# Window attention: the exponentials' product with the values in rounded parts, and one step later

## The chip, the cores and the metric

The kernel runs on one core of a Trainium2 chip. The metric is the device time of one execution in microseconds. TensorE is the matmul engine, VectorE, ScalarE and GpSimd the three elementwise ones, SyncE issues the transfers. The profile writes PE, DVE, ACT, POOL and SP for them, and PEld for TensorE's weight loads.

## The reference, cut to what matters

The model is a chain of blocks: an RWKV-7 time mixing, a stick-breaking attention, a window attention and a short convolution, each followed by a gated feed-forward network (f0 to f3). The change is in the window attention. It has 16 query heads of 64 features over 4 key and value heads, 512 tokens, and 256 context tokens that every query sees. Queries go in blocks of 128. A block of queries sees the keys at most 128 positions away, and a learned logit (the sink) takes part in the softmax without a value.

```python
def gqa_softmax(q, k, v, mask, sink):
    s = jnp.einsum('bkgqd,bkjd->bkgqj', q, k, preferred_element_type=jnp.float32) * (q.shape[-1] ** -0.5)
    if mask is not None:
        s = jnp.where(mask, s, NEG)
    ...
        sk = sink.astype(jnp.float32)[None, :, :, None, None]
        m = jnp.maximum(s.max(axis=-1, keepdims=True), sk)
        e = jnp.exp(s - m)
        p = e / (e.sum(axis=-1, keepdims=True) + jnp.exp(sk - m))
    return jnp.einsum('bkgqj,bkjd->bkgqd', p.astype(v.dtype), v)
```

## The kernel before

Activations lie with features on the partitions and tokens in the columns. A linear layer (`lin_pe`, L325) keeps weights and activations as two tensors of TensorE's rounded type: the rounded value (`hi`) and the rest (`lo`, the value minus its rounded value), and sums three products, hi by hi, hi by lo and lo by hi. ScalarE rounds each weight chunk (L295), VectorE makes its rest (L302). A matmul of plain `F32` tensors needs no such parts; the trace shows two records for each.

**The window attention** (L2491 to L2720) goes through 16 groups, one for each key head `kv` and query block `qb`. A group handles four query heads at once, 4 x 128 = 512 columns. It has `NQ` key blocks of 128: two of the context and two or three of the neighbourhood, so 4, 5, 5, 4 for the four `qb`. All engines follow one list written out by hand, `WATT` (L2520), in which every engine finds its own part of each step:

- `max` (g, j): TensorE makes the scores of head j of group g with queries on the partitions (L2572 to L2581, 512 or 640 columns), VectorE takes the maximum (L2670). It runs one group ahead. Two areas of PSUM take turns, so a `max` waits for VectorE's reduce two before it (L2570).
- `shift` (g): VectorE forms the negative maximum, bounded by the sink (L2679), and four diagonal matrices of it (L2683).
- `key` (g, q): TensorE makes the scores of key block q with keys on the partitions, from rounded keys and their rests (L2599, L2600), adds the mask where there is one (L2602) and the shift (L2605). ScalarE takes the exponential into `Pw` (L2643), `F32`, three buffers. The key step q = NQ gives the sink's part (L2592), whose exponential (L2636) goes into `dn`.
- `val` (g, q): TensorE multiplies `vw` by `Pw` (L2611). `vw` (L2093) holds 64 columns of values and 64 columns of ones, so the product gives both the weighted values and the sum of the exponentials. `vw` and `Pw` are `F32`. The value columns are written by ScalarE from PSUM (L2423), the ones by a GpSimd memset (L2480).
- `end` (g, 0..3): VectorE adds the denominators (L2691), ScalarE inverts them by Ln and Exp (L2649, L2651), VectorE normalises (L2697, two instructions), ScalarE rounds (L2655) and GpSimd makes the rest (L2719). In groups 5 to 12 VectorE also scales one part of the residual stream in `end` 3 (L2707).
- `queries` (g), in groups 0 to 3: ScalarE and VectorE split two more query blocks of the rotary embedding (`rope_hi`, `rope_lo`, L2373).

The list for step `_q` of a group puts `key`, then the next group's `max`, then `end` of the group before, then `val` of the key block one before:

```python
                WATT.append(("key", _g, _q))
                if _g + 1 < NG and _q < 4:
                    WATT.append(("max", _g + 1, _q))
                    ...
                if _g and _q < 4:
                    WATT.append(("end", _g - 1, _q))
                if _q:
                    WATT.append(("val", _g, _q - 1))
```

Each engine's queue is in order. VectorE's first instruction of the stage is L2660, TensorE's is the first `max` (L2572), which waits for ScalarE's last value copy. The output projection (`wino`) starts when GpSimd has the last rest (L2617).

Of the kernel before, what the change touches and what calls it, by code (L numbers as in the profile page):

```python
# [7 lines left out]
F32 = mybir.dt.float32  # L8
F32R = mybir.dt.float32r
# [228 lines left out]
def program(nc, d_h, d_ctx, d_vec, d_cst, d_csr, d_csb, d_csw, d_slc, d_w, d_ada, d_cond, d_out):  # L238
    with ExitStack() as ctx:
# [3 lines left out]
        def sig(name, order):  # L243
            return Sig(sem(name), order)
# [21 lines left out]
        def v(name, i=0, n=1):  # L266
            o = VEC[name] + i
            return vec[:, o:o + n]
# [206 lines left out]
        class Squares:  # L475
# [9 lines left out]
            def rest(self, e):  # L485
                e.preload_act_table_set("natural_log_exp_and_others")
                rms_square(e, self.t, self.src, self.sq, self.there, (6, 7))
# [1605 lines left out]
        vw = mem.left("vw", [128, 6, 4, 128])  # L2093
# [21 lines left out]
        r1 = mem.left("r1", [128, LX])  # L2115
        mem.lo = cx0
# [350 lines left out]
        def win_pool(e):  # L2467
# [12 lines left out]
            e.memset(vw[:, :, :, 64:128], 1.0).then_inc(*zeroed.up("vw", 0))  # L2480
# [15 lines left out]
        NP = 3  # L2496
        Pw = mem.left("Pw", [128, NP, 512])
        nmr = mem.left("nmr", [128, 2, 4], F32R)
# [4 lines left out]
        on = mem.left("on", [128, 2, 2, 128])  # L2503
        flatp = psum[:, :, :].rearrange("p b c -> p (b c)")
# [16 lines left out]
        for _g in range(NG):  # L2521
            for _q in range(NQ[_g] + 1):

                WATT.append(("key", _g, _q))
                if _g + 1 < NG and _q < 4:
                    WATT.append(("max", _g + 1, _q))
                    if _q == 3:
                        WATT.append(("shift", _g + 1, 0))
                if _g and _q < 4:
                    WATT.append(("end", _g - 1, _q))  # L2530
                if _q:
                    WATT.append(("val", _g, _q - 1))
            if _g < 4:

                WATT.append(("queries", _g, 6 + _g))
        WATT += [("end", NG - 1, q) for q in range(4)]
# [13 lines left out]
        t_p = sig("t_p", wk("key"))  # L2550
        t_v = sig("t_v", [(g, q) for g, q in wk("val")])
# [4 lines left out]

        def watt_pe(e):
            e.wait_ge(*q_v.at(2))
            for s, g, q in WATT:
# [46 lines left out]
                elif s == "val":  # L2606
                    b, n = 6 + g % 2, pkey[g, q]
                    e.wait_ge(*t_p.at(g, q))
                    if q == 0 and g >= 2:
                        e.wait_ge(*t_o.at(g - 2, 1))  # L2610
                    ins = e.matmul(psum[:, b, :], vw[:, ts_[q][0], kv, :], Pw[:, n % NP, :], start=q == 0, stop=q == NQ[g] - 1,  # L2611
                                   skip_group_check=True)
                    ins.then_inc(*t_v.up(g, q))
# [6 lines left out]
        def watt_act(e):  # L2620
# [4 lines left out]
            for s, g, q in WATT:  # L2625
# [4 lines left out]
                elif s == "key":  # L2630
# [10 lines left out]
                    if m >= NP:  # L2641
                        e.wait_ge(*t_v.at(*keys_[m - NP]))
# [15 lines left out]
        def watt_dve(e):  # L2658
            e.wait_ge(*w_used.at(last_chunk("winv", 0)))
            e.tensor_scalar(ns8[:, :], v("sink", 0, 16), -8.0, None, ALU.mult).then_inc(*t_n8.up(0))  # L2660
            for s, g, q in WATT:
# [22 lines left out]
                elif s == "queries":  # L2684
                    rope_lo(e, q)
                elif s == "end":
# [25 lines left out]
        def watt_pool(e):  # L2712
            for s, g, q in WATT:
                kv, qb = groups[g]
                i = g % 2
                if s == "end" and q == 3:
                    cs_ = slice(128 * qb, 128 * qb + 128)
                    e.wait_ge(*t_oh.at(g))
                    e.tensor_tensor(XoW.lo[:, 2 * kv:2 * kv + 2, cs_], on[:, i, :, :],  # L2719
                                    XoW.hi[:, 2 * kv:2 * kv + 2, cs_].bitcast(F32), ALU.subtract).then_inc(*t_ol.up(g))  # L2720
# [329 lines left out]
```

## Time and profile before

| | us |
|---|---|
| three runs | 3118.66 median (3114.68 to 3126.62) |
| the profiled execution, its own time | 3126.0 |
| its span in the profile | 3124.2 |
| TensorE busy | 3029.7 (97%) |
| VectorE busy | 1822.9 (58%) |
| ScalarE busy | 1309.7 (42%) |
| GpSimd busy | 519.5 (17%) |

The profile is of one execution. A span is counted from its first instruction. Busy time of TensorE is modelled: matmuls overlap in its pipeline, so the distance from one start to the next says more on the cost of a pass than its duration does. The window attention lies at about 1960 to 2125 us. The granted clock is a share of TensorE's full speed.

### The profile page before, as it was taken

The numbers are of one execution on the slowest core, as the hardware profiler recorded it, in microseconds if no ns is written. First come the engines' busy times: TensorE is split into PE (matmuls) and PEld (weight loads), VectorE is DVE, ScalarE is ACT, GpSimd is POOL, SyncE is SP. The second block draws the span as 40 slices with busy tenths as digits, with TensorE's granted clock in tenths as the row PEclk, the third lists the DMA queues.
The fourth block names the chain that finished last, engine by engine and source line by source line (L and its number), as shares of the span: only waits on it lengthen the run. The fifth ranks groups of instructions, "written<-read, shape, count | busy, mean of one in ns | idle before, by whom it ended". The sixth has DMA issues, their size and how long they took to land.

```text
span 3124.2 us, 46510 instructions
## 1 busy us (share of the span) xinstructions
PE 3029.7 (97%) x19324; PEld 2667.5 (85%) x19324; DVE 1822.9 (58%) x2664; ACT 1309.7 (42%) x2229; POOL 519.5 (17%) x464
## 2 busy tenths in 40 slices
PE   6999999999999999999999999998999999999999
PEld 6987878799999989998999987666888878878887
DVE  7675545448858563563876865664544543365353
ACT  4464555524323254673322355553332332343232
POOL 0002222123203200001311322101211201112020
PEclk9899989899999999999999999999999999999999
DMA  3210000014545422003554542101222222223222
GB/s 107 77 50 35 1 1 1 36 48 169 185 154 188 131 103 88 8 1 130 183 183 163 180 153 68 41 1 54 95 95 88 93 91 94 97 79 98 86 93 94
DMA packets 79554, 284.32 MB, mean 91 GB/s; under 512 B 8528, under 2 KB 9296, under 8 KB 78576
## 3 DMA queue, kind: packets, MB, share of 16 engines
q1 hardware_dynamic: 79344, 281.35, 27.1%
q8 instruction: 153, 2.51, 0.3%
q14 instruction: 57, 0.47, 0.1%
HBM read 274.96 MB, written 6.36 MB: 90 GB/s over the span
## 4 chain that ended last, share of the span: by engine, by line
PE 92%; DVE 4%; ACT 2%; issue 1%; DMA 0%; POOL 0%; SPq 0%; DVEq 0%; ACTq 0%; POOLq 0%
PE psum L345 64%; PE psum L2611 2%; PE psum L1193 2%; PE psum L839 2%; PE psum L1783 2%; PE psum L1214 2%; PE psum L1984 2%; PE psum L1225 1%; PE psum L1222 1%; PE psum L1966 1%; PE psum L1957 1%; PE psum L782 1%; DVE xt L682 1%; PE psum L2605 1%; PE psum L503 1%
## 5 line engine op out<-in xcount | busy, mean ns | idle before, releaser
L302 DVE TENSOR_TENSOR wlo<-wraw,whi 128x1024 fp32r<-128x1024 f32 (+2 forms) x398 | 508.6, 1299 | 629.7 <-ACT whi L295 620.6
L295 ACT CAST whi<-wraw 128x1024 fp32r<-128x1024 f32 (+2 forms) x398 | 396.2, 1022 | 515.4 <-PE psum L345 483.5
L426 DVE CUSTOM_DVE_ANT_0 araw<-araw,cond 128x1024 f32<-128x1024 f32 x112 | 181.2, 1655 | 0.0
L345 PE MATMUL psum<-f0xh,whi 128*128 128x264 f32 x704 | 143.8, 286 | 5.5 <-DVE f0xl L540 3.9
L345 PE MATMUL psum<-f1xh,whi 128*128 128x258 f32 x704 | 142.4, 284 | 5.6 <-DVE f1xl L540 3.8
L345 PE MATMUL psum<-f2xh,whi 128*128 128x512 f32 x352 | 140.1, 398 | 4.2 <-DVE f2xl L536 4.2
L345 PE MATMUL psum<-f3xh,whi 128*128 128x512 f32 x352 | 139.9, 397 | 4.2 <-DVE f3xl L536 4.2
L345 PE MATMUL psum<-f0xh,wlo 128*128 128x264 f32 x704 | 143.4, 285 | 0.0
L345 PE MATMUL psum<-f0xl,whi 128*128 128x264 f32 x704 | 143.0, 285 | 0.0
L345 PE MATMUL psum<-f1xh,wlo 128*128 128x258 f32 x704 | 142.3, 284 | 0.0
L345 PE MATMUL psum<-f1xl,whi 128*128 128x258 f32 x704 | 141.9, 283 | 0.0
L345 PE MATMUL psum<-f2xl,whi 128*128 128x512 f32 x352 | 139.9, 397 | 0.0
L345 PE MATMUL psum<-f2xh,wlo 128*128 128x512 f32 x352 | 139.7, 397 | 0.0
L345 PE MATMUL psum<-f3xl,whi 128*128 128x512 f32 x352 | 139.6, 397 | 0.0
L345 PE MATMUL psum<-f3xh,wlo 128*128 128x512 f32 x352 | 139.5, 396 | 0.0
L1301 ACT ACTIVATE XX<-psum 128x512 fp32r<-128x512 f32 (+2 forms) x216 | 109.4, 519 | 31.1 <-PE psum L1225 25.2
L1345 DVE TENSOR_TENSOR WW<-psum,csr 128x256 fp32r<-128x256 f32 (+1 forms) x216 | 84.0, 395 | 54.7 <-PE psum L1214 53.3
L345 PEld LDWEIGHTS psum<-f0xh,whi 128*128 128x128 f32 x704 | 109.8, 190 | 6.1 <-issue 4.3
L345 PEld LDWEIGHTS psum<-f1xh,whi 128*128 128x128 f32 x704 | 109.6, 191 | 6.2 <-issue 4.2
L345 PEld LDWEIGHTS psum<-f1xh,wlo 128*128 128x128 f32 x704 | 109.7, 190 | 0.0
L345 PEld LDWEIGHTS psum<-f0xh,wlo 128*128 128x128 f32 x704 | 109.6, 190 | 0.0
L345 PEld LDWEIGHTS psum<-f0xl,whi 128*128 128x128 f32 x704 | 109.5, 189 | 0.0
(509 smaller groups left out, 8605.7 us busy)
## 6 DMA issues: line engine op xcount, KB each, us to landing
wraw<-d_w SPq DMA_DIRECT2D x357, 512.0 KB, 3.3
araw<-d_ada SPq DMA_DIRECT2D x112, 512.0 KB, 3.3
wraw<-d_w SPq DMA_DIRECT2D x32, 384.0 KB, 3.4
hn<-d_h SPq DMA_DIRECT2D x4, 528.0 KB, 7.6
hres<-d_h SPq DMA_DIRECT2D x1, 2112.0 KB, 8.5
spill<-hres SPq DMA_DIRECT2D x1, 2112.0 KB, 7.4
hres<-spill SPq DMA_DIRECT2D x1, 2112.0 KB, 9.1
cond<-d_cond SPq DMA_DIRECT2D x2, 1024.0 KB, 4.8
```

Of the source, the lines that this page charges most:

```text
L295: e.copy(whi[0:rows, n % NH, 0:kt * cols], wraw[0:rows, n % NR, 0:kt * cols]).then_inc(*w_hi.up(n))
L302: e.tensor_tensor(wlo[0:rows, n % NH, 0:kt * cols], wraw[0:rows, n % NR, 0:kt * cols], whi[0:rows, n % NH, 0:kt * cols].bitcast(F32), ALU. ...
L345: ins = e.matmul(psum[0:bw, b0 + nb * len(sl) + si, 0:ln], l_ if z == 2 else h_, (xp.lo if z == 1 else xp.hi)[:, k, o:o + ln], start=k == ...
L426: e.tensor_tensor_reduce(out=w, in0=w, in1=self.c[:, col, :], scale=1.0, scalar=0.0, op0=ALU.mult, op1=ALU.add, accum_out=ada[:, ly, blk, ...
L839: ins = e.matmul(psum[0:ln, b, 256 * (ti % 2):256 * (ti % 2) + 256], a_, w_[:, i, :], start=k == 0 and z == 0 and ti % 2 == 0, stop=k == 7 ...
L1193: ins = e.matmul((p1, p0)[w].rearrange("p (a t) -> p a t", a=4)[:, :, 0:T], src[:, blk, q.tok], q.Zp[:, :, 0:T], start=True, stop=True)
L1214: ins = e.matmul(p1[:, 128 * j:128 * j + T], q.Ar[0:T, j, 0:T], q.X[0:T, j, 0:T], start=True, stop=True)
L1301: e.activation(q.X[0:T, o:4, 0:T], p0.rearrange("p (j x) -> p j x", j=4)[:, o:4, 0:T], ACT.Copy).then_inc(*c_xe.up(blk, c, s[1]))
L1345: e.tensor_tensor(q.W[0:T, :, 0:T], p1[:, 0:256].rearrange("p (j x) -> p j x", j=2)[:, :, 0:T], q.bc(lv(s[1])), ALU.mult).then_inc(*c_we.u ...
L1783: ins = e.matmul(psum[0:ln, b, 256 * (ti % 2):256 * (ti % 2) + 256], a_, w_[:, k - k0, :], start=k == 0 and z == 0 and ti % 2 == 0, stop=k ...
L1984: ins = e.matmul(psum[:, 6 + half, lo_ - a0:hi_ - a0], vz, wtt[:, w % 2, col + lo_ - a:col + hi_ - a], start=kb == 2 and hh % 2 == 0, stop ...
L2611: ins = e.matmul(psum[:, b, :], vw[:, ts_[q][0], kv, :], Pw[:, n % NP, :], start=q == 0, stop=q == NQ[g] - 1, skip_group_check=True)
```

## The change

The value product is made of three rounded passes. `vw` becomes a rounded tensor, and VectorE makes its rest `vwl` in three subtractions from PSUM, and zeros for the columns of ones (rest of 1 is 0), ahead of its part of the list. GpSimd copies each exponential into a rounded tensor `Ph` (four buffers), VectorE subtracts it from `Pw` into `Pl` (four buffers), and TensorE multiplies `vw` by `Ph`, `vwl` by `Ph` and `vw` by `Pl`. The exponentials' buffer is free when its rest is made; a copy waits for the value product four blocks back. The list gets a part `rest`, `val` follows its scores by two key blocks in place of one, and all but the fourth `end` move one step later. GpSimd's columns of ones become a copy, and it makes the rest of the heads' outputs (`rest(g - 2)`) before the first copy of a group.

```diff
@@ -2090,7 +2090,7 @@
         mem.lo = sb0
-        vw = mem.left("vw", [128, 6, 4, 128])
+        vw = mem.left("vw", [128, 6, 4, 128], F32R)
         csw = mem.left("csw", [128, NCSW])
@@ -2477,7 +2478,8 @@
             e.wait_ge(*w_ss.at("B"))
-            e.memset(vw[:, :, :, 64:128], 1.0).then_inc(*zeroed.up("vw", 0))
+            e.tensor_copy(vw[:, :, :, 64:128].rearrange("p t h x -> p (t h) x"),
+                          ones[:, 0:64].unsqueeze(1).broadcast_to((128, 24, 64))).then_inc(*zeroed.up("vw", 0))
             for n in range(10):
@@ -2493,14 +2495,24 @@
         ns8 = mem.left("ns8", [128, 16])
-        NP = 3
+
+        NP, NPR = 3, 4
         Pw = mem.left("Pw", [128, NP, 512])
+        Ph = mem.left("Ph", [128, NPR, 512], F32R)
         nmr = mem.left("nmr", [128, 2, 4], F32R)
 ...
         on = mem.left("on", [128, 2, 2, 128])
+        assert mem.lo <= wx1
+
+        mem.lo = cx0
+        vwl = mem.left("vwl", [128, 6, 4, 128], F32R)
+        Pl0 = mem.left("Pl0", [128, 2, 512], F32R)
+        assert mem.lo <= rp0
+        mem.lo = rp1
+        Pl1 = mem.left("Pl1", [128, 2, 512], F32R)
         flatp = psum[:, :, :].rearrange("p b c -> p (b c)")
@@ -2526,14 +2538,18 @@
                         WATT.append(("shift", _g + 1, 0))
-                if _g and _q < 4:
-                    WATT.append(("end", _g - 1, _q))
+                if _g and _q == 0:
+                    WATT.append(("val", _g - 1, NQ[_g - 1] - 1))
+                if _g and _q:
+                    WATT += [("end", _g - 1, x) for x in ((_q - 1,) if _q < 4 else (3,) if _q == 4 else ())]
                 if _q:
-                    WATT.append(("val", _g, _q - 1))
+                    WATT.append(("rest", _g, _q - 1))
+                if _q > 1:
+                    WATT.append(("val", _g, _q - 2))
             if _g < 4:
 ...
                 WATT.append(("queries", _g, 6 + _g))
-        WATT += [("end", NG - 1, q) for q in range(4)]
+        WATT += [("val", NG - 1, NQ[-1] - 1)] + [("end", NG - 1, q) for q in range(4)]
         wk = lambda name: [(g, q) for s, g, q in WATT if s == name]
@@ -2548,14 +2564,21 @@
         t_p = sig("t_p", wk("key"))
+        t_ph = sig("t_ph", keys_)
+        t_pl = sig("t_pl", wk("rest"))
+        t_vl = sig("t_vl", [(b,) for b in range(4)])
         t_v = sig("t_v", [(g, q) for g, q in wk("val")])
 ...
 
+        def Pl(n):
+            return (Pl1 if n % NPR >= 2 else Pl0)[:, n % 2, :]
+
         def watt_pe(e):
             e.wait_ge(*q_v.at(2))
+            e.wait_ge(*t_vl.at(2))
             for s, g, q in WATT:
@@ -2604,13 +2627,17 @@
                 elif s == "val":
-                    b, n = 6 + g % 2, pkey[g, q]
-                    e.wait_ge(*t_p.at(g, q))
+                    b, n, t = 6 + g % 2, pkey[g, q], ts_[q][0]
+                    if n == 0:
+                        e.wait_ge(*t_vl.at(3))
+                    e.wait_ge(*t_ph.at(g, q))
                     if q == 0 and g >= 2:
                         e.wait_ge(*t_o.at(g - 2, 1))
-                    ins = e.matmul(psum[:, b, :], vw[:, ts_[q][0], kv, :], Pw[:, n % NP, :], start=q == 0, stop=q == NQ[g] - 1,
-                                   skip_group_check=True)
-                    ins.then_inc(*t_v.up(g, q))
+                    e.matmul(psum[:, b, :], vw[:, t, kv, :], Ph[:, n % NPR, :], start=q == 0, stop=False, skip_group_check=True)
+                    e.matmul(psum[:, b, :], vwl[:, t, kv, :], Ph[:, n % NPR, :], start=False, stop=False, skip_group_check=True)
+                    e.wait_ge(*t_pl.at(g, q))
+                    e.matmul(psum[:, b, :], vw[:, t, kv, :], Pl(n), start=False, stop=q == NQ[g] - 1,
+                             skip_group_check=True).then_inc(*t_v.up(g, q))
 
@@ -2639,7 +2666,7 @@
                     if m >= NP:
-                        e.wait_ge(*t_v.at(*keys_[m - NP]))
+                        e.wait_ge(*t_pl.at(*keys_[m - NP]))
                     e.activation(Pw[:, m % NP, :], psum[:, 4 + n % 2, :], ACT.Exp, scale=0.125).then_inc(*t_p.up(g, q))
@@ -2658,6 +2685,13 @@
             e.tensor_scalar(ns8[:, :], v("sink", 0, 16), -8.0, None, ALU.mult).then_inc(*t_n8.up(0))
+
+            for b in range(3):
+                e.wait_ge(*q_v.at(b))
+                e.tensor_tensor(vwl[:, 2 * b:2 * b + 2, :, 0:64], psum[:, b, :].rearrange("p (t h x) -> p t h x", t=2, h=4),
+                                vw[:, 2 * b:2 * b + 2, :, 0:64].bitcast(F32), ALU.subtract).then_inc(*t_vl.up(b))
+            e.tensor_scalar(vwl[:, :, :, 64:128].rearrange("p t h x -> p (t h) x"),
+                            ones[:, 0:64].unsqueeze(1).broadcast_to((128, 24, 64)), 0.0, None, ALU.mult).then_inc(*t_vl.up(3))
             for s, g, q in WATT:
@@ -2683,6 +2717,12 @@
                     rope_lo(e, q)
+                elif s == "rest":
+                    n = pkey[g, q]
+                    e.wait_ge(*t_ph.at(g, q))
+                    if n >= NPR:
+                        e.wait_ge(*t_v.at(*keys_[n - NPR]))
+                    e.tensor_tensor(Pl(n), Pw[:, n % NP, :], Ph[:, n % NPR, :].bitcast(F32), ALU.subtract).then_inc(*t_pl.up(g, q))
                 elif s == "end":
@@ -2710,14 +2750,22 @@
         def watt_pool(e):
-            for s, g, q in WATT:
+            def rest(g):
                 kv, qb = groups[g]
-                i = g % 2
-                if s == "end" and q == 3:
-                    cs_ = slice(128 * qb, 128 * qb + 128)
-                    e.wait_ge(*t_oh.at(g))
-                    e.tensor_tensor(XoW.lo[:, 2 * kv:2 * kv + 2, cs_], on[:, i, :, :],
-                                    XoW.hi[:, 2 * kv:2 * kv + 2, cs_].bitcast(F32), ALU.subtract).then_inc(*t_ol.up(g))
+                cs_ = slice(128 * qb, 128 * qb + 128)
+                e.wait_ge(*t_oh.at(g))
+                e.tensor_tensor(XoW.lo[:, 2 * kv:2 * kv + 2, cs_], on[:, g % 2, :, :],
+                                XoW.hi[:, 2 * kv:2 * kv + 2, cs_].bitcast(F32), ALU.subtract).then_inc(*t_ol.up(g))
+
+            for n, (g, q) in enumerate(keys_):
+                if q == 0 and g >= 2:
+                    rest(g - 2)
+                e.wait_ge(*t_p.at(g, q))
+                if n >= NPR:
+                    e.wait_ge(*t_v.at(*keys_[n - NPR]))
+                e.tensor_copy(Ph[:, n % NPR, :], Pw[:, n % NP, :]).then_inc(*t_ph.up(g, q))
+            rest(NG - 2)
+            rest(NG - 1)
 
```

The hunk left out only keeps an address (`rp1`).

## Rows read from the trace of the kernel before

**Rows 1.** Busy per engine in the stage: length, PE, PEld, DVE, ACT, POOL, clock.
```profile
1967.00:2121.00 154.00, 152.92 (x642) 104.55 (x642) 99.79 (x198) 88.35 (x189) 11.00 (x15) 0.98 0.06 21
```

**Rows 2.** Waits in the stage: us in total, times, longest.
```profile
DVE mxw L2670 <- PE psum L2581: 37.5, 42, 2.7
```

**Rows 3.** Line L2592: durations in ns, first and last start.
```profile
L2592 PE MATMUL psum<-dg,oR x16: 792/793/799, 1977.1 to 2118.9; 128*128 128x512 f32 x16
```

**Rows 4.** TensorE's timeline, one step: start us, us, line.
```profile
2031.45 0.39 PE L2602 MATMUL psum<-mk,iR 128*128 128x512 f32 x1
2031.68 0.39 PE L2605 MATMUL psum<-dg,oR 128*128 128x512 f32 x1
2031.90 0.28 PE L2572 MATMUL psum<-Kh,Qx 128*128 128x256 f32 x1
...
2032.20 1.07 PE L2611 MATMUL psum<-Pw,vw 128*128 128x512 f32 x2
...
2033.57 0.39 PE L2605 MATMUL psum<-dg,oR 128*128 128x512 f32 x1
```

**Rows 5.** VectorE's groups from 1966 to 2121, by form: busy us, mean ns.
```profile
L2670 DVE TENSOR_REDUCE mxw<-psum 128x1 f32<-128x640 f32 x32 | 26.4, 824 | 19.8 <-PE psum L2581 19.6
L2670 DVE TENSOR_REDUCE mxw<-psum 128x1 f32<-128x512 f32 x28 | 19.3, 691 | 18.1 <-PE psum L2581 17.9
L2683 DVE TENSOR_SCALAR dg<-cst,nmr 128x128 fp32r<-128x128 f32 x64 | 14.0, 283 | 0.6
L2697 DVE TENSOR_TENSOR on<-psum,rdn 64x256 f32<-64x256 f32 x30 | 12.5, 418 | 3.0 <-ACT rdn L2651 2.1
L2691 DVE TENSOR_TENSOR dn<-psum,dn 64x512 f32<-64x512 f32 x16 | 11.1, 695 | 5.5 <-ACT dn L2636 5.0
L2679 DVE SCALAR_TENSOR_TENSOR nmr<-mxw,ns 128x4 fp32r<-128x4 f32 x16 | 7.6, 475 | 0.5
L2707 DVE SCALAR_TENSOR_TENSOR hres<-hres,vec,r 128x512 f32<-128x512 f32 x8 | 6.0, 747 | 0.0
L2373 DVE TENSOR_TENSOR Qx<-qw,Qx 64x512 fp32r<-64x512 f32 x8 | 5.5, 686 | 6.8 <-ACT Qx L2359 6.6
```

**Rows 6.** Groups of instructions over the whole span, by form: VectorE, then GpSimd.
```profile
L2047 DVE TENSOR_TENSOR spl<-za,sph 128x512 fp32r<-128x512 f32 x16 | 10.9, 682 | 0.0
...
L1680 POOL TENSOR_TENSOR f2hidl<-f2C,f2hidh 128x512 fp32r<-128x512 f32 x22 | 28.7, 1302 | 16.1 <-ACT f2hidh L1614 16.1
...
L1369 POOL COPY ZP<-RA 64x256 f32<-64x256 f32 x32 | 12.6, 393 | 0.1
...
L1369 POOL COPY ZP<-RA 64x32 f32<-64x32 f32 x8 | 1.6, 200 | 0.0
```

**Rows 7.** ScalarE's timeline: the exponential of the step of rows 4.
```profile
2032.10 0.60 ACT L2643 ACTIVATE Pw<-psum 128x512 f32<-128x512 f32 x1
```

**Rows 8.** Timelines of TensorE and VectorE at the stage's start.
```profile
1961.47 0.39 PE L2572 MATMUL psum<-Kh,Qx 128*128 128x256 f32 x1
...
1962.17 1.23 DVE L2660 TENSOR_SCALAR ns<-vec 128x16 f32<-128x16 f32 x1
1963.31 2.62 DVE L2670 TENSOR_REDUCE mxw<-psum 128x1 f32<-128x512 f32 x4
```

**Rows 9.** Timelines of VectorE and GpSimd: the shift alone and beside GpSimd.
```profile
1965.97 0.16 DVE L2679 SCALAR_TENSOR_TENSOR nmr<-mxw,ns 128x4 fp32r<-128x4 f32 x1
...
2035.02 0.70 DVE L2679 SCALAR_TENSOR_TENSOR nmr<-mxw,ns 128x4 fp32r<-128x4 f32 x1
...
2034.97 0.73 POOL L2719 TENSOR_TENSOR Qx<-on,Qx 128x256 fp32r<-128x256 f32 x1 [9.32 <-ACT Qx L2655]
```

**Rows 10.** As rows 1, in stretches of 2 us at the start.
```profile
1964.00:1966.00 2.00, 1.65 (x8) 1.06 (x8) 1.91 (x4) 0.00 (x0) 1.87 (x2) 1.00 0.00 0
1966.00:1968.00 2.00, 0.90 (x3) 0.81 (x4) 1.01 (x5) 0.07 (x1) 0.00 (x0) 0.60 0.00 0
...
1972.00:1974.00 2.00, 2.00 (x8) 1.30 (x7) 0.06 (x1) 0.09 (x1) 0.00 (x0) 0.69 0.00 0
```

More of the change, by code:

```diff
@@ L2115, in program @@
         r1 = mem.left("r1", [128, LX])
+        rp1 = mem.lo
         mem.lo = cx0
```

## The prediction

> **What bounds the kernel now.** I first read the busy time of each engine over the attention, from the first dense matmuls to the last value product [rows 1]: TensorE is busy for 152.9 of 154.0 us, VectorE for 99.8, ScalarE for 88.4, GpSimd for 11.0. So TensorE sets the pace here, and VectorE, at 65%, is the only other engine worth counting. The waits say the same from the other side: VectorE stood for 37.5 us in 42 waits for score matmuls [rows 2]. TensorE hardly waits. The 16 denominator matmuls, one for each group of heads and queries, start from 1977.1 to 2118.9 [rows 3], so a group takes 141.8 / 15 = 9.45 us. A group has four or five key blocks (4, 5, 5, 4 for the query blocks of each of four head groups), 72 in all.
>
> The timeline of TensorE gives the price of each pass in one step [rows 4]. A rounded pass of 512 columns starts 0.23 us after the one before it (L2602 to L2605). The maximum's matmuls take from 2031.90 to 2032.20, 0.30 us; with 640 columns more, and I take 0.40 as the mean. From 2032.20 to the next L2605 at 2033.57 lie the unrounded value product and two rounded passes, so the unrounded product costs 1.37 - 0.47 = 0.90 us.
>
> **What the change takes away.** Three rounded passes cost 0.70 us in place of 0.90, on the engine that is the bound. 72 x 0.20 = 14 us less of TensorE's work. If nothing else were late, that is the gain.
>
> **What it adds on VectorE.** One subtraction of 128x512 from two SBUF tensors for each key block. The same operation stands elsewhere in this kernel at 682 ns [rows 6] (L2047). 72 x 0.682 = 49.1 us. VectorE's own forms in the stage [rows 5] sum to 102.4 us: reduces 45.7, the diagonals 14.0, the normalisation 12.5, the denominators 11.1, shifts 7.6, residual scaling 6.0, query rests 5.5. With the rests it has 151.5 us to do, and about 0.03 us between two instructions on some 200 of them makes 157. The stage took 155. So VectorE alone, never waiting for anything, needs as long as the stage takes today: the 14 us can't be had. This floor is the firmest number of the forecast.
>
> **What it adds on GpSimd.** 72 copies of 128x512 to the rounded type. No row has that form. GpSimd's copies of 256 and 32 columns take 393 and 200 ns [rows 6], 0.86 ns for a column more, so 0.61 us for 512; from below 0.39 us, from above 1.30 us, its two-input form of 512 columns [rows 6] (L1680). I take 0.6, since a copy is nearer to the copies' rows. That is 43 us on an engine with 11 us of work, off the path by its sum; 1.3 would make 94, still under the stage.
>
> **Where VectorE's queue stops TensorE.** VectorE runs in order, and the order by steps is: maximum 0; maximum 1, denominator, rest 0; maximum 2, rest 1; maximum 3, shift, four diagonals, two normalisations, rest 2; residual, rest 3 (and rest 4). TensorE takes the third pass of block q two steps after its scores. I follow one group around until it closes. Prices: reduce 0.75 (mean of the two forms) + 0.03, shift 0.33, diagonals 0.82, normalisations 0.90, denominator 0.72, rest 0.71, all from [rows 5, 6]. A hand-over from TensorE takes 0.19 us: L2605's slot ends at 2031.91 and the exponential starts at 2032.10 [rows 4, 7]. Back to TensorE I allow 0.1.
>
> Four key blocks: after the maximum of step 3, VectorE needs 0.78 + 0.33 + 0.82 + 0.90 + 0.71 = 3.54 us to reach the end of rest 2. TensorE has 1.4 us to do in that time (value 1, denominator, two passes of value 2) and then stops. Then it does the third pass, key 0, maximum 0, value 3, key 1, maximum 1: 0.23 + 0.70 + 0.40 + 0.70 + 0.70 + 0.40 = 3.13. VectorE answers with reduce, denominator, rest 0: 2.21. TensorE goes on with the third pass, key 3 (half the time with a mask) and maximum 3: 0.23 + 0.82 + 0.40 = 1.45. With four hand-overs, 0.6, the loop is 10.9 us. Five key blocks: the same VectorE stretches, 5.75; TensorE 0.23 + 0.23 + 0.70 + 0.70 + 0.40 + 0.70 + 0.70 + 0.40 = 4.06, then 0.23 + 0.70 + 0.40 = 1.33; hand-overs 0.6: 11.7. The mean is 11.3, against 9.45: 1.85 us more for each group. The last group has no maximum or shift of a next one and gets 0.5, so 14 x 1.85 + 0.5 = 26.4 us. TensorE stands twice in each group, before a third pass: 2.4 us (1.7 with five blocks) and 0.9.
>
> The eight residual scalings (0.75 us, [rows 5], L2707) lie in slack in groups of four blocks; in the four groups with five they delay rest 3, which value 3 is about to need: 4 x 0.6 = 2.4 us. The two buffers' waits that are new (the exponential waits for a rest three blocks back, the copy for a value product four back) come due at least a microsecond after their release in this loop, so I cost them at nothing.
>
> **Start and end.** TensorE began at 1961.47, as soon as ScalarE had the values [rows 8]. Now VectorE's three subtractions from PSUM stand before it, 3 x 0.69 (the price of L2691's form), in the queue behind L2660, which ended at 1963.4; then the zeroing of 128x1536, for which I take 1.0 to 1.75 us, by the diagonals' 283 ns for 128 columns (a few long ones can't be cheaper than a third of 12 of them). The first reduce at 1963.31 [rows 8] moves to about 1967.3: 4.0 us. At the end the last block passes through GpSimd and VectorE, 0.6 + 0.7, but the denominator's exponentials, which take as long, run beside it: 0.5.
>
> **GpSimd against VectorE.** A shift (L2679) takes 0.16 us alone, and 0.70 us when it starts 0.05 us after a GpSimd subtraction of 0.73 us: it ends just after that one [rows 9]. So an instruction of VectorE with two SBUF inputs stood behind GpSimd's. In the loop the copy of block 2 starts about 0.1 us before rest 0, which is on the path; a full wait is 0.5 us, 15 times 7.5 us. The copies of the other blocks meet reduces, which read PSUM. Between 0 and 7.5 I take 4.
>
> The Trainium skill (SBUF — State Buffer, "SBUF: two separate sides") speaks against the change here: it says that VectorE with two SBUF inputs and GpSimd hold one port pair by turns, each for a whole instruction. By that rule the sum would have 7.5 us in this place, and without a lock 0. The trace agrees, by the shift's 0.70 us.
>
> **Sum.** 26.4 + 2.4 + 4.0 + 0.5 + 4 = 37.3 us. The profiled execution took 3126.0 us, which would become 3163; it lies 7.3 above the median of three, 3118.66, so the forecast for the median is 3156 us.
>
> **The rivals.**
> - *GpSimd is the slow link* (0.15). Its copy takes 1.3 us and every rest waits behind a copy or loses the port to one, about 1.1 us more in each group, 16 us: 3172. For it: L1680's row; against it: the copy's row. The Trainium skill (GPSIMD Engine Reference, "Performance versus the Vector engine") gives 769 ns for 512 elements in the best loop; the sum with that price would be 2 to 3 us higher.
> - *The clock falls in the stalls* (0.17). The granted clock went from full speed (2.4 GHz) to half (1.2 GHz) at 1966 to 1968, after TensorE had stood more than it had worked since 1962: it is busy for 1.65 us of 1964 to 1966 and for 0.90 of 1966 to 1968, and the clock is back only within 1972 to 1974 [rows 10]. The changed loop has a stall of up to 2.4 us in each group. The loop holds 4.6 us of TensorE's passes on its path; at half speed they cost 4.6 more. In one group of three that is 22 us: 3178; in all of them 3220. Against it: by the passes counted above TensorE works for 8.3 of 11.3 us, far more than at 1964 to 1968.
> - *VectorE's floor only* (0.10). The two key blocks of slack take up the bursts and VectorE never stands: 157 instead of 155 us, and 4.0 at the start, 3125 to 3128. Against it: two reduces of a group wait for maxima that TensorE issues only after a third pass.
> - *TensorE stays the bound* (0.06). The other side: rests are done in time everywhere, and the stage loses 14 us and pays 4.5 at start and end, 3109; with nothing paid at the start it would be under 3103 in part of these cases. It decides if VectorE's total stays under some 140 us, a rest at 0.5 us or less. The subtraction's row at 682 ns, sixteen times, speaks against it.
>
> **How the numbers follow.** The loop as worked out has 0.52. Unknown in it: the port from 0 to 7.5, the zeroing 0.4 either way, and the loop itself, which I trust to a quarter of its 26 us; 3145 to 3168. The clock and GpSimd cases reach to 3188; below, 3132 leaves out the floor and the TensorE case, 0.16, and above it a clock that is low in most groups, 0.03. About 0.5% (16 us) is what a measurement of this kernel tells from no change. The floor (0.10) and 0.04 of TensorE's case lie within it, the other 0.02 below 3103: faster 0.02, same 0.14, slower 0.84, which is all the rest.
>
> **What would show it.** Right: the denominator matmuls of groups are 11 to 11.5 us apart; TensorE is busy under 80% of the stage with its waits before the third passes put down to the rests on VectorE; VectorE is above 85%; the first reduce is 4 us later; no difference outside the stage. Wrong: VectorE waits for GpSimd's copies more than for matmuls (first rival), a granted clock under 0.9 in the stage (second), VectorE above 95% (third), TensorE above 97% (fourth).

## The result, and the profile after

The changed kernel takes 3172.51 us (median of 4 runs, 3166.96 to 3175.77), the kernel before, run beside it, 3120.51 us (4 runs, 3114.68 to 3126.62). The medians are 52 us apart. The ratio on record is 1.0155, with a 95% interval of 1.0136 to 1.0174; it is not the quotient of the two medians (1.0167), and by it the loss is 48 us (42 to 54). The profiled execution has an own time of 3175.77 us and a span of 3174.0 us.

The first view is again the busy time of the engines over the stage, from the first denominator matmul to the last. It answers to [rows 1]; columns are length, TensorE, its weight loads, VectorE, ScalarE, GpSimd, granted clock.

```profile
1986.00:2168.00 182.00, 147.49 (x675) 113.33 (x673) 143.16 (x261) 86.49 (x182) 58.62 (x83) 0.95 0.05 18
```

TensorE, which hardly stood before, is busy for 81% of the stage. VectorE is at 79%, so it isn't full either: the two wait for each other. The denominator matmuls, against [rows 3]:

```profile
L2615 PE MATMUL psum<-dg,oR x16: 391/395/403, 1986.1 to 2167.2; 128*128 128x512 f32 x16
```

A group takes 181.1 / 15 = 12.07 us, 9.45 before. The waits of the stage (us in total, times, longest), against [rows 2]:

```profile
POOL Ph L2766 <- ACT Pw L2670: 115.7, 70, 6.4
...
PEld psum L2639 <- DVE Pl L2725: 51.6, 38, 2.5
DVE mxw L2704 <- PE psum L2604: 35.5, 39, 2.7
PE psum L2639 <- DVE Pl L2725: 35.3, 34, 2.1
...
DVE Pl L2725 <- POOL Ph L2766: 0.6, 1, 0.6
```

The weight load of the third value pass (L2639) waits for VectorE's rest 38 times, a little over twice in each group, and VectorE waits as long as before for the scores. The rests themselves wait for GpSimd's copy once. GpSimd's 115.7 us are idle time of an engine that nobody waits for.

The groups of VectorE and GpSimd, by form (busy us, mean ns, idle before), against [rows 5, 6]:

```profile
L2725 DVE TENSOR_TENSOR Pl<-Pw,Ph 128x512 fp32r<-128x512 f32 x72 | 52.9, 752 | 1.5 <-POOL Ph L2766 0.6
...
L2747 DVE SCALAR_TENSOR_TENSOR hres<-hres,vec,r 128x512 f32<-128x512 f32 x8 | 9.7, 1218 | 0.0
...
L2713 DVE SCALAR_TENSOR_TENSOR nmr<-mxw,ns 128x4 fp32r<-128x4 f32 x16 | 3.3, 207 | 0.5
L2691 DVE TENSOR_TENSOR vwl<-psum,vw 128x512 fp32r<-128x512 f32 x3 | 1.9, 676 | 0.0
L2693 DVE TENSOR_SCALAR vwl<-cst 128x1536 fp32r<-128x1536 f32 x1 | 1.6, 1646 | 0.0
```

```profile
L2766 POOL CAST Ph<-Pw 128x512 fp32r<-128x512 f32 x72 | 49.3, 685 | 118.5 <-ACT Pw L2670 115.7 <-PE psum L2639 2.8
```

How the two engines wait for each other is seen in one group of four key blocks. TensorE's timeline (start, us, line; in brackets the idle time before), some instructions of it:

```profile
2083.87 0.40 PE L2637 MATMUL psum<-Ph,vwl 128*128 128x512 f32 x1
2086.35 0.50 PE L2639 MATMUL psum<-Pl,vw 128*128 128x512 f32 x1 [2.08 <-DVE Pl L2725]
...
2091.63 0.40 PE L2637 MATMUL psum<-Ph,vwl 128*128 128x512 f32 x1
2092.39 0.50 PE L2639 MATMUL psum<-Pl,vw 128*128 128x512 f32 x1 [0.36 <-DVE Pl L2725]
```

VectorE's timeline beside it:

```profile
2082.87 0.82 DVE L2704 TENSOR_REDUCE mxw<-psum 128x1 f32<-128x640 f32 x1 [0.57 <-PE psum L2604]
2083.72 0.16 DVE L2713 SCALAR_TENSOR_TENSOR nmr<-mxw,ns 128x4 fp32r<-128x4 f32 x1
2083.92 0.87 DVE L2717 TENSOR_SCALAR dg<-cst,nmr 128x128 fp32r<-128x128 f32 x4
2084.71 0.86 DVE L2737 TENSOR_TENSOR on<-psum,rdn 64x256 f32<-64x256 f32 x2
2085.60 0.69 DVE L2725 TENSOR_TENSOR Pl<-Pw,Ph 128x512 fp32r<-128x512 f32 x1
2086.21 1.23 DVE L2747 SCALAR_TENSOR_TENSOR hres<-hres,vec,r 128x512 f32<-128x512 f32 x1
...
2090.06 0.82 DVE L2704 TENSOR_REDUCE mxw<-psum 128x1 f32<-128x640 f32 x1 [1.14 <-PE psum L2604]
2090.91 0.70 DVE L2731 TENSOR_TENSOR dn<-psum,dn 64x512 f32<-64x512 f32 x1
2091.64 0.69 DVE L2725 TENSOR_TENSOR Pl<-Pw,Ph 128x512 fp32r<-128x512 f32 x1
```

The five-block group behind it shows the stalls of the other form:

```profile
2097.68 0.50 PE L2639 MATMUL psum<-Pl,vw 128*128 128x512 f32 x1 [1.44 <-DVE Pl L2725]
...
2099.42 0.50 PE L2639 MATMUL psum<-Pl,vw 128*128 128x512 f32 x1 [0.53 <-DVE Pl L2725]
```

Between the maximum at 2082.87 and the third pass at 2086.35 VectorE works without a gap, and the rest that TensorE needs is the last of five things. Then TensorE has the scores to catch up with, and VectorE waits for those, 1.14 us at 2090.06.

The clock, in stretches of 4 us (columns as in the first view). At [rows 1] it was 0.98 over the stage, and full after 1978.

```profile
2018.00:2022.00 4.00, 2.84 (x13) 2.05 (x13) 3.64 (x10) 2.18 (x6) 0.94 (x2) 1.00 0.00 0
2022.00:2026.00 4.00, 3.12 (x11) 2.68 (x12) 3.75 (x6) 2.14 (x4) 1.41 (x2) 0.67 0.00 0
...
2038.00:2042.00 4.00, 4.00 (x18) 3.44 (x18) 1.30 (x2) 0.90 (x2) 0.95 (x2) 0.70 0.00 0
2074.00:2078.00 4.00, 4.00 (x17) 3.43 (x15) 1.50 (x3) 1.19 (x2) 0.61 (x1) 0.57 0.00 0
```

It goes to the lower of its two levels (1.2 GHz) for part of five groups; the other two places are 2110 to 2118 and 2134 to 2142. A group with such a place is 1.6 us longer than the same group of experiment 3, where the clock stays full (13.32 against 11.74, 16.18 against 14.60, 13.33 against 11.76, 10.51 against 8.95, 16.16 against 14.61), 7.8 us together. The other ten differ by 0.2 us or less. In 2074 to 2078 a granted clock of 0.57 is the lower level for 3.4 of the 4 us, so 1.7 us of work at full speed is lost there.

**Where the 52 us are.** In the profiled executions the way from the first value copy on ScalarE to the last denominator matmul (I call it the stretch) went from 1959.8 to 2118.9 before and goes from 1966.5 to 2167.2 now: 159.1 and 200.7, so 41.6 us more. From there to the output projection it is 0.8 more. The own times differ by 49.8; 6.7 of it lie ahead of the stretch, where the code is the same but for GpSimd's columns of ones. That start varies from profile to profile, over 1952.5 to 1971.9, also between kernels that are the same up to there, so the 6.7 need not be the change's. The stretch and its end give 42.4 us, at the lower edge of the interval of 42 to 54; the medians' 52 are some 10 us more, which stays open.

### The profile page after: what moved, and what is told of

It is laid out like the page before. It is cut to its first block, busy times and chain, and to the rows that moved or that the text cites. A ratio compares the mean times of both kernels' runs of the same rounds, so it can differ in the third digit from the quotient of the medians.

```text
span 3174.0 us, 46939 instructions
## 1 busy us (share of the span) xinstructions
PE 3041.0 (96%) x19396; PEld 2689.5 (85%) x19396; DVE 1874.7 (59%) x2740; ACT 1312.2 (41%) x2229; POOL 572.0 (18%) x536
## 4 chain that ended last, share of the span: by engine, by line
PE 90%; DVE 6%; ACT 2%; issue 1%; DMA 0%; POOL 0%; DVEq 0%; SPq 0%; ACTq 0%; POOLq 0%
PE psum L345 63%; PE psum L1193 2%; PE psum L839 2%; PE psum L1783 2%; PE psum L1214 2%; PE psum L1984 2%; PE psum L1225 1%; PE psum L1222 1%; PE psum L1966 1%; PE psum L1957 1%; PE psum L782 1%; DVE Pl L2725 1%; PE psum L2639 1%; DVE xt L682 1%; PE psum L2309 1%
## 5 line engine op out<-in xcount | busy, mean ns | idle before, releaser
L426 DVE CUSTOM_DVE_ANT_0 araw<-araw,cond 128x1024 f32<-128x1024 f32 x112 | 181.1, 1654 | 0.0
L345 PEld LDWEIGHTS psum<-f1xl,whi 128*128 128x128 f32 x704 | 110.1, 191 | 0.0
```

Of the source, the lines that this page charges most:

```text
L345: ins = e.matmul(psum[0:bw, b0 + nb * len(sl) + si, 0:ln], l_ if z == 2 else h_, (xp.lo if z == 1 else xp.hi)[:, k, o:o + ln], start=k == ...
L426: e.tensor_tensor_reduce(out=w, in0=w, in1=self.c[:, col, :], scale=1.0, scalar=0.0, op0=ALU.mult, op1=ALU.add, accum_out=ada[:, ly, blk, ...
```

## The experiments

Line numbers in the expectations and diffs are those of the changed kernel. After each median stands the ratio to the kernel before, run beside it (median 3123.75 us for experiments 1 to 4, 3124.07 for 5 to 8, 3123.71 for 9 to 11), with its 95% interval. The period is the mean distance of the denominator matmuls.

**1. No rests on VectorE.** The exponentials' rests are left out: the third pass multiplies the rounded part once more. The exponentials' buffer is then free as soon as its copy is made.

```diff
-                    e.wait_ge(*t_pl.at(g, q))
-                    e.matmul(psum[:, b, :], vw[:, t, kv, :], Pl(n), ...
+                    e.matmul(psum[:, b, :], vw[:, t, kv, :], Ph[:, n % NPR, :], ...
```

> The third pass takes the rounded exponentials again in place of their rests, and VectorE makes no rests; TensorE's passes, GpSimd's copies and the order are those of the change. It leaves out the exponentials' rests. If VectorE's rests and their place in its queue are the cost, the stage is TensorE's again: 14 us less than before for the passes, 3 to 4 more at the start, 3108 to 3116 us, groups 8.6 to 8.9 us apart. If GpSimd's copies are the slow link, little goes away and it stays above 3145.

Measured: 3115.1 us (10 runs), 0.9985 [0.997, 0.9999]. Group period 8.81 us, stretch 151.7.

```profile
1987.00:2119.00 132.00, 131.01 (x671) 108.95 (x670) 91.07 (x191) 85.28 (x180) 52.34 (x81) 1.00 0.07 25
```

TensorE is full again, with three passes and GpSimd's copies in place. All of the loss goes with VectorE's 72 rests, and the gain on TensorE is real: 9.45 - 8.81 = 0.64 us a group, 9.6 us in 15. The list alone gives 0.10 of the 0.64 (experiment 2).

**2. The new order alone.** The kernel before, with the new list and a fourth exponential buffer, its product still unrounded.

```diff
-        NP = 3
+        NP = 4
...
-                if _g and _q < 4:
-                    WATT.append(("end", _g - 1, _q))
+                if _g and _q == 0:
+                    WATT.append(("val", _g - 1, NQ[_g - 1] - 1))
...
-                    WATT.append(("val", _g, _q - 1))
+                    WATT.append(("val", _g, _q - 2))
```

> The kernel before with the change's list alone (value product two key blocks behind, ends one step later, four buffers of exponentials), unrounded product. If only VectorE's rests cost, it is the kernel before, 3118 to 3124 us. If the later ends or the later product cost by themselves (the denominator and its inversion come later than they are needed), 3130 or more.

Measured: 3119.79 us (10 runs), 0.9994 [0.9975, 1.0013]. Period 9.35, stretch 156.7. The second block of lag costs nothing.

**3. A filled stall.** TensorE adds passes with zero weights before the third pass of block 2.

```diff
+                    for _ in range((7 if NQ[g] == 4 else 5) if q == 2 and g < NG - 1 else 0):
+                        e.matmul(psum[:, b, :], zz[:, :], Ph[:, n % NPR, :], start=False, stop=False, ...)
                     e.wait_ge(*t_pl.at(g, q))
```

> The changed kernel with 7 (5 in groups of five key blocks) more passes of TensorE with zero weights in the longest stall, before the third pass of key block 2, 1.2 to 1.6 us of a stall of 1.4 to 2.1. If the falls of the granted clock cost what the long groups show (five of them, 1.6 to 2.1 us each, 9 us), the clock stays at full speed and the time is 3160 to 3167 us. If the clock costs nothing because VectorE sets the pace, 3171 to 3175. If the fillers delay the path, more than 3176.

Measured: 3155.32 us (4 runs), 1.0115 [1.0096, 1.0134]. Period 11.56, stretch 193.0.

```profile
1979.00:2152.00 173.00, 158.79 (x758) 122.70 (x756) 141.84 (x256) 85.64 (x180) 58.54 (x82) 1.00 0.05 19
```

More work on TensorE makes the kernel faster: the clock stays full, and the stretch is 7.7 us shorter, which is what the five long groups lose against these (7.8). So the loop with a full clock has a period of 11.56. The 1.6 to 2.1 us of the expectation set groups beside others of another kind; like by like it is 1.6. The median came below the 3160 to 3167 expected.

**4. The rest first.** In each step VectorE makes the rest ahead of the next group's maximum, not at the end.

```diff
                 WATT.append(("key", _g, _q))
+                if _q:
+                    WATT.append(("rest", _g, _q - 1))
                 if _g + 1 < NG and _q < 4:
...
-                if _q:
-                    WATT.append(("rest", _g, _q - 1))
```

> The changed kernel with one move in the list: in each step VectorE makes the rest ahead of the next group's maximum (and so ahead of shift, diagonals and normalisation). By the loop, rests 0 and 2 leave VectorE's answers to a maximum, and the pace goes towards VectorE's own work of 9.8 us for a group plus hand-overs, 10.2 to 10.7 us: 3142 to 3155 us. If only VectorE's total counted and its order did not, 3170 as the changed kernel. If GpSimd's copies are late, a rest placed first holds up the maxima and it is slower than 3175.

Measured: 3135.39 us (4 runs), 1.0048 [1.0032, 1.0065]. Period 9.89, stretch 168.1.

```profile
1977.00:2125.00 148.00, 136.10 (x669) 108.18 (x668) 138.21 (x255) 84.43 (x179) 60.93 (x82) 0.99 0.06 22
```

```profile
PEld psum L2639 <- DVE Pl L2725: 17.1, 20, 2.4
```

The same instructions in another order take 37 us less in the medians. Period and median came below what was expected (10.2 to 10.7, 3142 to 3155). The waits fall from 51.6 to 17.1 us, and VectorE is 93% busy, so by its sum this version is near VectorE's floor; experiment 8 tests that.

**5. ScalarE rounds.** ScalarE takes the exponential twice, into the rounded and the plain buffer; GpSimd copies nothing.

```diff
+                    e.activation(Ph[:, m % NPR, :], psum[:, 4 + n % 2, :], ACT.Exp, scale=0.125).then_inc(*t_ph.up(g, q))
                     e.activation(Pw[:, m % NP, :], psum[:, 4 + n % 2, :], ACT.Exp, scale=0.125).then_inc(*t_p.up(g, q))
```

> The changed kernel without GpSimd's 72 copies: ScalarE takes the exponential twice from PSUM, once into the rounded tensor and once into the plain one. VectorE's work and order stay. If VectorE's queue is the cost, it is the changed kernel but for the waits at the shared port, 3164 to 3174 us; the residual scalings should take 0.75 instead of 1.22 us only where no other GpSimd work is beside them. If GpSimd's copies or the port hold up the path, 0.5 us or more for each group comes back, 3150 to 3162. If ScalarE becomes late, slower than 3178.

Measured: 3172.4 us (4 runs), 1.0145 [1.0116, 1.0175], as the changed kernel. Period 12.14. The second exponential (0.60 us) stands in the chain where the copy (0.62) stood, so the chain is as long; what is gone is most of GpSimd's work beside VectorE. It did cost a little, which the clock hides. The granted clock fell in seven groups here (its first low windows of 4 us start at 2028, 2040, 2088, 2104, 2116, 2140 and 2152), not in five. The three groups with a fall only here are 4.2 us longer together than in the changed kernel. The twelve others are 1.7 us shorter, like by like (the eighth fell only in the changed kernel, so experiment 3's length is its measure). The residual scalings take 1224 ns as before, since GpSimd's subtraction for the heads' outputs still stands beside them. So VectorE's order sets the pace, and the copies' share is, as an estimate from these 1.7 us, some 2 us of the stretch.

**6. The rest ahead of the shift only.** It stands behind the maximum, but ahead of shift, diagonals and normalisation.

```diff
+                if _q:
+                    WATT.append(("rest", _g, _q - 1))
                 if _g + 1 < NG and _q == 3:
                     WATT.append(("shift", _g + 1, 0))
```

> The changed kernel with rest 2 moved ahead of shift, diagonals and normalisation only; in all steps the rest still stands behind the maximum. The first stretch of VectorE, 3.5 us before the third pass of block 2, becomes 1.5 and its stall of TensorE vanishes; the diagonals and the normalisation then come 0.7 us later, which key 0 and the end can bear. By the loop 1.2 to 1.5 us less for a group, and without long stalls no fall of the clock (9 us): 3142 to 3152 us. If the place of rest 0 behind the maximum and the denominator is what costs, little changes: above 3160.

Measured: 3146.72 us (4 runs), 1.0063 [1.0043, 1.0083]. Period 10.34, stretch 174.7. So the one long block of work (shift, diagonals, normalisations) ahead of rest 2 carries 26 of the 37 us, the maxima ahead of the other rests the remainder. Of the 26, 18 are the period against experiment 3's 11.56, the rest is the clock, which is full here too.

**7. One block behind.** All as changed, but the value product follows its scores by one block.

```diff
-                if _q > 1:
-                    WATT.append(("val", _g, _q - 2))
+                if _q:
+                    WATT.append(("val", _g, _q - 1))
```

> The changed kernel with the value product one key block behind the scores, as before the change; rests, copies and the ends' places stay. From the scores of a block to its third pass lie the exponential, the copy and the rest, 2.2 us with hand-overs, and a maximum of VectorE before them, against 1.6 us of TensorE's own work: 0.7 to 1.2 us more in most steps, 3 to 5 us for a group, 3205 to 3240 us. If the second block of lag hides nothing, since VectorE's total sets the pace, 3172 to 3180.

Measured: 3248.06 us (4 runs), 1.0382 [1.0362, 1.0403]. Period 17.31, stretch 285.8, clock 0.87 in it.

```profile
PEld psum L2637 <- DVE Pl L2723: 110.1, 58, 3.4
```

Slower than expected (3205 to 3240). The chain from exponential through copy and rest to the third pass is in the open at every block, and the clock falls more often.

**8. A lighter VectorE.** Experiment 4, with the diagonals made by ScalarE and no zero columns in `vwl`: the second pass writes 64 columns' outputs.

```diff
-                    e.matmul(psum[:, b, :], vwl[:, t, kv, :], Ph...
+                    e.matmul(psum[0:64, b, :], vwl[:, t, kv, 0:64], Ph...
...
+                        e.activation(dg[:, i, j, :], ident, ACT.Copy, scale=nmr[:, i, j:j + 1].bitcast(F32)).then_inc(...)
```

> The kernel with the rest first, and besides: the four diagonals on ScalarE, and no zero columns (the second pass takes the 64 value columns alone and writes 64 partitions). VectorE's work for a group falls from 9.8 to 8.9 us, TensorE's is 8.3 to 8.6. If VectorE's total is what is left of the loss, the groups are 9.0 to 9.4 us apart and the time is 3116 to 3126 us. If key 0 now waits for ScalarE's diagonals, behind the exponential of block 3, it stays at 3130 or above.

Measured: 3133.32 us (10 runs), 1.0018 [1.0003, 1.0034]. Period 9.91, stretch 165.6. VectorE is busy for 85% now, but the period is that of experiment 4. The waits (us, times, longest) show what took its place:

```profile
PEld psum L2637 <- DVE Pl L2722: 15.8, 24, 1.6
DVE Pl L2722 <- POOL Ph L2763: 13.3, 17, 1.1
...
PEld psum L2628 <- ACT dg L2658: 8.8, 7, 1.7
```

The diagonals are ahead of an exponential in ScalarE's queue, so exponential, copy and rest come later by them. A miss: VectorE has less work, and nothing was gained. That doesn't show that its sum is not what holds experiment 4, since the diagonals' new place costs by itself.

**9. The third pass later.** The changed kernel, its rests where they were; the third pass is issued one block after the first two, and the ends of the group before move one block down with it (that part of the edit is not shown).

```diff
                 if _q > 1:
                     WATT.append(("val", _g, _q - 2))
+                if _q > 2:
+                    WATT.append(("third", _g, _q - 3))
```

> Edit: the changed kernel, with the third pass of each key block (the one that takes the rest) issued one block later than its first two passes; the ends of the previous group move one block down with it. The rests stay where the change puts them in VectorE's queue. If the wait for the rests is only a matter of lateness (a rest comes some 2 us late, once or twice a group), a block more of lag (some 2 us) covers it: period of a group 9.4 to 10.2 us, median 3130 to 3145 us. If VectorE's own queue is a loop that the lag cannot open (its maxima wait for TensorE, which waits for its rests), the waits come back one step later: period 11 to 12 us, median 3155 to 3172 us.

Measured: 3133.59 us (10 runs), 1.0028 [1.0012, 1.0044]. Period 9.96, stretch 168.7. The wait for the rests (51.6 us in the changed kernel), and the engines' busy time:

```profile
PEld psum L2645 <- DVE Pl L2731: 14.2, 20, 1.7
...
1974.00:2123.00 149.00, 137.41 (x670) 107.25 (x668) 140.33 (x256) 84.79 (x178) 62.50 (x82) 1.00 0.06 22
```

The rests stand where they stood in VectorE's queue, and 42 of the 52 us are gone. So it is a matter of lateness, which either an earlier rest or a later use mends. VectorE is 94% busy here, as in experiment 4: what is left is near its sum.

**10. Both.** Rest first, and third pass later.

> Edit: both, the rests ahead of the next group's maximum and the third pass one block later. The kernel with the rests first waited 17 us for rests and had VectorE 93% busy. If nothing is left but VectorE's own work (138 us in 148), the period falls from 9.89 to 9.2 to 9.5 us and the median to 3124 to 3130 us; if the waits only change place, 3133 to 3138 us, as before.

Measured: 3141.79 us (4 runs), 1.007 [1.0043, 1.0096]. Period 10.40, stretch 175.4. Slower than either alone. The waits of TensorE's loads:

```profile
PEld psum L2626 <- ACT dn L2669: 13.9, 8, 1.9
PEld psum L2632 <- DVE dg L2723: 13.4, 10, 2.3
...
PEld psum L2645 <- DVE Pl L2731: 0.2, 1, 0.2
```

The wait for the rests is gone (0.2 us). In its place the scores wait for the diagonals, which now stand behind a rest, and for ScalarE to free their bank. The expectation for changed places was 3133 to 3138; it came higher.

**11. All of it.** Experiment 10, with the lighter VectorE of experiment 8.

> Edit: rests first, the third pass one block later, the four diagonals of a group on ScalarE, and no zero columns beside the rounded values' rest (its pass writes 64 columns' worth of outputs). VectorE has some 115 us of work, TensorE 124 to 130. If the wait for rests was all that held the lighter kernel at 9.91 us a group, TensorE is the bound again: period 8.9 to 9.3 us, median 3112 to 3120 us, below the kernel before (ratio 0.996 to 0.999). If ScalarE's queue (diagonals 1.3 us, then denominators 1.1) delays the scores' exponentials and the chain to the third pass, the lag covers that too; if instead the scores wait for the diagonals, the period stays at 9.7 to 10 us and the median at 3130 to 3135 us.

Measured: 3166.53 us (6 runs), 1.0135 [1.0111, 1.0159]. Period 11.67. A clear miss. The waits:

```profile
ACT dg L2664 <- DVE nmr L2719: 29.0, 14, 2.8
...
PEld psum L2626 <- ACT Pw L2678: 21.1, 10, 3.3
```

ScalarE stands in its queue at the diagonals, waiting for the shift, and the exponentials behind them come late by that; TensorE then waits for a bank of scores. The granted clock is 0.95 in the stage as well. No version here beats the kernel before with all its work done; the nearest are experiments 8 (1.0018) and 9 (1.0028), which their intervals don't tell apart.

## Why the prediction was right

Side and mechanism were right: TensorE and VectorE wait for each other in the loop that was named. The likeliest figure, 3156, was 16 us short. 3172.51 lies above the 3145 to 3168 of the loop case and within the whole range of 3132 to 3188 only by what the clock and GpSimd rivals added to it, so that the range held is in part luck. By its steps:

- **What TensorE gains.** Forecast 14 us. Experiment 1 gives 9.6 us of period over 15 groups, 1.5 of them by the list alone: 0.12 us for a key block, not 0.20. Three rounded passes take 0.75 us in the group shown (2087.90 to 2088.65), for 0.70.
- **The closed loop.** The forecast was 11.3 us for a group, and with the last group's 9.95, residual scaling 2.4 and port 4 over 15 periods (14 x 11.3 + 9.95 + 6.4) / 15 = 11.64. Experiment 3, with the clock full, has 11.56; from shift to shift, the loop as it was closed, it is 11.69 for (14 x 11.3 + 6.4) / 14 = 11.76. This was the largest term, and it held, but the nearness is partly luck. The stalls of the group shown are 2.08 and 0.36 us before the same two third passes that were named, for 2.4 and 0.9, and from the third pass to the awaited maximum it takes 3.71 us, for 3.13 and a hand-over of 0.19. In experiment 3 the last period is 6.23 us (6.92 before), not 9.95, and the 14 others are 11.94 in the mean, not 11.76. Experiments 4, 6, 7 and 9 show that it is the rests' place against their use, and not VectorE's sum: nearly the same sum takes 9.89, 10.34, 17.31 and 9.96 us a group in them, 12.07 in the changed kernel.
- **The residual scaling.** 0.6 us in each of four groups of five blocks, before the third pass of block 3. That stall is 0.53 us at 2099.42, and it is missing in the groups of five without a scaling (2000.58, 2161.80).
- **The terms inside it.** VectorE's rest takes 752 ns in the mean (0.68 alone) for 682. GpSimd's copy takes 0.62 us where nothing is beside it, for 0.61, and 685 ns in the mean. The port was to cost 4 us, between 0 and 7.5; experiment 5 puts the copies' share at some 2. At 2091.64 the rest came first and GpSimd's copy was the one that lasted 1.12 us.
- **The port elsewhere.** The residual scaling rose from 747 to 1218 ns: at 2086.21 it stood beside GpSimd's 0.80 us subtraction. The shift fell from 475 to 207 ns, since it no longer meets one. The Trainium skill (SBUF — State Buffer, "SBUF: two separate sides") has VectorE with two SBUF inputs and GpSimd hold the port pair by turns. The trace agrees in who waits, by these rows; of the 7.5 us that the prediction drew from the rule, experiment 5, which takes the copies away, shows some 2.
- **The start.** VectorE's first maximum was to come 4.0 us later. It starts 6.8 us after the first value copy, 3.5 before: 3.3. The three rests took 1.87 us and the zeroing 1.65, within its 1.0 to 1.75. The first denominator matmul is 2.3 us later, counted from the value copy. In these 2.3 lies a low clock that lasts longer: added up from the windows of 2 us, some 10 us at 1972 to 1984 for some 7 before ([rows 10] and the windows between).
- **The end.** 0.8 for 0.5.
- **The step that was mis-sized: the clock.** The forecast's likeliest case had it full and gave its fall a chance of 0.17, at 4.6 us for each affected group, 22 us for one in three. It did fall, in five of 15 periods, and cost 1.6 us each, 7.8 us; experiment 3 took back 7.7 in the stretch. The price was too high because it took the whole group's passes at half speed, where a low stretch covers only some of them. The reading that made a fall look unlikely was wrong too: TensorE had not stood more than it had worked before the fall at 1966, it was busy for 0.67 + 1.65 us of the 4 before.

```profile
1962.00:1964.00 2.00, 0.67 (x4) 0.53 (x4) 2.00 (x4) 0.25 (x2) 1.92 (x3) 1.00 0.00 0
```

- **The sum.** Loop (11.56 x 15 - 141.8) 31.6, clock 7.7, start 2.3, end 0.8: 42.4 us, for 37.3. The rest of the medians' 52 lies in no term.

Of the rivals, GpSimd as the slow link fell (one wait of 0.6 us for its copy; experiment 5), VectorE's floor fell (79% busy), and TensorE as the bound fell; experiment 1 shows the time that this last one would have given, had the rests cost nothing. The waits stand where the prediction put them, before the third passes and for the rests. Four other signs of being right missed, if narrowly: 12.07 us between denominators for 11 to 11.5, TensorE at 81% for under 80, the first maximum 3.3 us later for 4, and VectorE at 79% for above 85. The last was too high even for the loop forecast: 143 us of work stand in 182, and would be 82% of 15 x 11.64.

## What to carry to other kernels

When an operation is added on an engine with room, ask first where in that engine's queue it stands and how long after that its result is used, then for the engine's sum: here nearly the same sum was worth anything from 10 us (experiment 9) to 124 (experiment 7). A closed loop of two in-order queues can be priced by hand from the trace of before: the whole came within 0.1 us in 11.6, but terms in it were off by 0.3 to 0.5 us (the last group by 3.7), and they cancelled. Lag in the list and an earlier place in the queue both cover a late result, but they don't add up: each moves something else behind, and the next late thing (here diagonals and a bank of scores) has to be named before both are applied.

## What was not expected of the hardware

- A loop whose TensorE stands 2 us once a group was granted the lower clock in five groups of 15, though TensorE worked 81% of the time. In one of them it was busy for 2.84 of the 4 us before the fall, while 2.56 us of 1998 to 2002 were followed by none. Which groups it takes was not found.
- Filling a stall with passes of zero weights paid: 12% more matmuls in the stage's window (758 for 675), 17 us less in the medians (12 by the two ratios), 7.7 of them in the stretch. The other 9.5 us are not explained by any row here, and neither are the 10 us by which the changed kernel's median exceeds its stretch. Each pair of medians has four runs on the changed side, and what lies ahead of the stretch varies by up to 19 us among the profiles.
- ScalarE makes a 128x128 diagonal in 391 ns (experiment 8), VectorE in 282 ns (experiment 5). The same rest on VectorE that takes 0.68 us alone took up to 1.23 us beside GpSimd.
